# A decoder layer with product-key experts: the 512 prompt tokens taken in two chunks, the dense layer of the second placed between the expert gathers of the first

## What is computed

```
mod  = silu(c) @ w_mod + b_mod                  # shift, scale and gain, six of them
z    = modulate(rmsnorm(x)) @ w_in              # xr, gr, q, k, v, two gates
y_r  = (rglru(causal_conv(xr)) * gelu(gr)) @ w_rnn_out
y_a  = window_attention(rope(q), rope(k), v) @ w_attn_out
x1   = x + gt1 * ((sig(gate_r) * y_r + sig(gate_a) * y_a) @ w_out)
h2   = modulate(rmsnorm(x1))
s    = (h2 @ w_pq) . sub_keys                   # 8 heads, two sides of 128 keys
      per head: best 16 of each side, best 16 of the 256 sums -> 16 experts, softmax shares
out  = sum over the 128 experts of a token: share * gelu(h2 . u_tab[e]) * v_tab[e]
y    = rmsnorm(x1 + gt2 * out)
```

## Time and profile before

| | |
|---|---|
| median of 3 runs | 2475.72 us (2469.61 to 2476.45) |
| span of the profiled execution | 2483.4 us |
| busy: PE, DVE, POOL, ACT | 1922.2, 1273.5, 1287.2, 706.2 us |
| first expert gather issued | 903.87 us |
| moved by transfers | 635.52 MB, of it gathers 545.33 MB |

### The profile page before, as it was taken

How to read it: one execution, slowest core, us unless ns; L and a number is a source line. 1 busy time by engine, 2 the same in 40 slices (tenths; PEclk the granted TensorE clock), 3 DMA queues, 4 the chain that set the end, 5 groups by cost and what they waited for, 6 DMA issues and landing times.

```text
span 2483.4 us, 25659 instructions
## 1 busy us (share of the span) xinstructions
PE 1922.2 (77%) x8102; PEld 1260.9 (51%) x8102; DVE 1273.5 (51%) x2896; ACT 706.2 (28%) x1770; POOL 1287.2 (52%) x1126
## 2 busy tenths in 40 slices
PE   8899988999997986676667757757767666776676
PEld 8899888888997972232223323323223222332232
DVE  2430366434333107656656746655756655765663
ACT  1222422233223323323313323222313323323222
POOL 0221123001431346667676766767767667766663
PEclk8899988999998997888878878788888888878877
DMA  5233332112221238999999999999999998999996
GB/s 222 94 131 111 123 136 97 39 47 82 86 86 35 77 134 334 366 363 360 362 332 357 373 342 363 361 339 340 366 356 358 354 351 327 369 354 358 372 347 233
DMA packets 164900, 635.52 MB, mean 256 GB/s; under 512 B 18800, under 2 KB 19640, under 8 KB 156224
## 3 DMA queue, kind: packets, MB, share of 16 engines
q0 software_dynamic: 149760, 545.33, 58.7%
q1 hardware_dynamic: 15072, 89.24, 10.1%
HBM read 631.30 MB, written 5.20 MB: 256 GB/s over the span
## 4 chain that ended last, share of the span: by engine, by line
PE 41%; issue 19%; DVE 15%; POOL 8%; DMA 6%; another core or an unknown queue 5%; ACT 5%; POOLq 0%; DVEq 0%; ACTq 0%; SPq 0%
PE acc L722 9%; POOL arena L1443 8%; PE acc L512 6%; PE acc L513 6%; PE acc L514 6%; DVE arena L1396 6%; DMA arena<-in_u_tab,pku 5%; PE acc L528 4%; PE acc L496 3%; ACT arena L996 2%; PE acc L562 2%; ACT pk L991 1%; PE acc L631 1%; PE acc L649 1%
## 5 line engine op out<-in xcount | busy, mean ns | idle before, releaser
L722 PE MATMUL acc<-arena 128*128 128x512 f32 x2080 | 1048.5, 668 | 473.6 <-ACT arena L996 346.8
L722 PEld LDWEIGHTS acc<-arena 128*128 128x128 f32 x2080 | 442.8, 217 | 1080.7 <-issue 1078.9
L1396 DVE CUSTOM_DVE_ANT_0 arena<-arena 128x1024 f32<-128x1024 f32 x520 | 631.2, 1226 | 416.0 <-DMA arena<-in_u_tab,pku 378.4
L1443 POOL DMA_INDIRECT arena<-in_v_tab,pku x520 | 552.9, 1063 | 316.3 <-issue 157.6
L1443 POOL DMA_INDIRECT arena<-in_u_tab,pku x520 | 526.2, 1012 | 167.3 <-issue 152.2
L1460 POOL TENSOR_TENSOR w_lo<-arena,w_hi 128x1024 fp32r<-128x1024 f32 x80 | 194.6, 2437 | 682.1 <-ACT w_hi L794 682.1
L512 PE MATMUL acc<-h_hi,w_hi 128*128 128x260 f32 x992 | 292.7, 295 | 22.0 <-DVE h_lo L1101 11.7
L513 PE MATMUL acc<-h_lo,w_hi 128*128 128x260 f32 x992 | 287.9, 290 | 0.0
L514 PE MATMUL acc<-h_hi,w_lo 128*128 128x260 f32 x992 | 287.1, 289 | 0.0
L988 ACT ACTIVATE pk<-pk 128x8 f32<-128x8 f32 x65 | 13.6, 209 | 936.3 <-issue 617.6
L512 PEld LDWEIGHTS acc<-h_hi,w_hi 128*128 128x128 f32 x992 | 194.4, 196 | 25.7 <-DVE h_lo L1101 12.6
(11 more groups left out here) (230 smaller groups left out, 1863.0 us busy)
## 6 DMA issues: line engine op xcount, KB each, us to landing
arena<-w_mod SPq DMA_DIRECT2D x24, 1024.0 KB, 4.9
arena<-in_u_tab,pku POOLq DMA_INDIRECT x520
arena<-in_v_tab,pku POOLq DMA_INDIRECT x520
arena<-w_pq SPq DMA_DIRECT2D x8, 1024.0 KB, 4.7
arena<-w_xr SPq DMA_DIRECT2D x5, 1024.0 KB, 4.9
arena<-w_gr SPq DMA_DIRECT2D x5, 1024.0 KB, 4.9
arena<-w_qk SPq DMA_DIRECT2D x5, 1024.0 KB, 4.7
arena<-w_rnn SPq DMA_DIRECT2D x8, 640.0 KB, 4.0
```

Source lines behind the costliest of these rows:

```text
L722: mm = pe.matmul(y[:, h, :], diag[q][:, j, :], vt_row[j][:, h * 512:(h + 1) * 512], start=False, stop=True, skip_group_check=True)
L1396: dve.tensor_tensor_reduce(u_row[j], u_row[j], hcur, 1.0, 0.0, ALU.mult, ALU.add, dots[q][:, j:j + 1]).then_inc(s_urd, 1)
L1443: pool.indirect_dma_start(out=row, out_offset=None, in_=table, in_offset=bass.IndirectOffsetOnAxis(ap=idx, axis=0), **more).then_inc(signa ...
```

## The change

The whole order of the kernel is written out, without hardware loops. Tokens go in two chunks: A has prompt tokens 0 to 255, B has 256 to 511 and the sample tokens. The dense layer is done for A alone, up to its first expert scores, then for B, whose instructions are dealt out among the expert groups of A on every engine. Every weight but those of the modulation is read twice, in pieces of 512 KB. Rows, scores and residuals that outlive a chunk go through memory (`x_rows`, `h_rows`, `key_rows`, through three small buffers that ACT fills and SP stores) and are read back when they are needed.

The plan lists the products of PE in their order (391 of them) with a cost for each. From the first scores of A on, each expert group has four **parts**. `_limits` deals the products out so that each of the 120 parts of the first 30 groups gets an equal share of the cost up to the first half of B's scores, and each of the next 20 parts an equal share of the rest. On each engine a part is: the expert work of two of the eight rows, then the dense steps up to the limit. A step of another engine carries the number of the product that it follows, and is done in the part in which that product is. In the dealt-out stretch there are four weight buffers and two `w_hi`; before it, eight and four.

The diff rewrites nearly every line; this is its core.

```
+def _rounding():
...
+    for n, p in enumerate(SPLITS):
+        over = max(free[p], HI_AFTER[p])
+        m = min([m for m in points if m + 1 >= over]) if n >= OWN_HI + EXTRA_HI else -1
+        assert m < FIRST[p], p
+        at.append(max(m, at[-1] if at else -1))
+    return at
...
+    for (lo, hi), steps in (((PEER_FROM, HALF_WAY), HALF_STEP), ((HALF_WAY, NPRODUCTS), LAST_STEP - HALF_STEP)):
+        total, spent, at = sum(COST[lo:hi]), 0.0, lo
+        for i in range(steps * PARTS):
+            goal = total * (i + 1) / (steps * PARTS)
+            while at < hi and spent + COST[at] / 2 <= goal:
+                spent += COST[at]
+                at += 1
+            limits.append(hi if i == steps * PARTS - 1 else at)
...
+        class Course:
...
+            def until(self, limit):
+                while self.at < limit:
+                    self.at = next(self.steps, NPRODUCTS)
...
         @block.tensor
...
+            def expert_sums(g, js):
+
+                tile, part, first, last = group_of(g)
+                if js[0] == 0:
+                    pe.wait_ge(s_diag, g + 1)
+                    if first and tile:
+                        pe.wait_ge(s_yfree, tile)
+                for j in js:
+                    pe.wait_ge(s_vt[j], 16 * (g + 1))
+                    for h in range(2):
+                        mm = pe.matmul(y[:, h, :], diag[g % 2][:, j, :], vt_row[j][:, h * 512:(h + 1) * 512],
+                                       start=(first and j == 0), stop=True, skip_group_check=True)
+                    mm.then_inc(s_vrd, 1)
...
+            for g in range(GROUPS + 2):
+                for q in range(PARTS):
+                    if g:
+                        expert_sums(g - 1, (2 * q, 2 * q + 1))
+                    if g * PARTS + q < len(LIMITS):
+                        course.until(LIMITS[g * PARTS + q])
...
         @block.scalar
...
+            def round_pieces(product):
+
+                while split[0] < len(SPLITS) and ROUND_AT[split[0]] <= product:
+                    piece = SPLITS[split[0]]
+                    src = await_piece(act, piece)
+                    if HI_AFTER[piece]:
+                        act.wait_ge(s_ready, HI_AFTER[piece])
+                    act.copy(w_hi[HI_SLOT[piece]], src[:, 0:D]).then_inc(s_hi, 1)
+                    split[0] += 1
...
+            for g in range(GROUPS + 2):
+                tile, step = divmod(g - 1, 2 * PH)
+                if g > 1 and step == 0:
+                    take_sums(tile - 1)
+                if g:
+                    weights(g - 1)
...
         @block.vector
...
+                for q in range(PARTS):
+                    if g <= GROUPS:
+                        dot_products(g, (2 * q, 2 * q + 1))
...
+                    if q == 1 and g % 2 == 0 and g // 2 + 1 <= HEADS:
+                        choose(g // 2 + 1)
...
         @block.gpsimd
...
+            def gather_v(g, j):
+                if g == 0:
+                    pool.wait_ge(s_ready, EXTRA_OVER)
+                else:
+                    pool.wait_ge(s_vrd, SLOT * (g - 1) + j + 1)
...
+            def dense():
+                for n, p in enumerate(SPLITS):
+                    yield max(ROUND_AT[n], 0)
+                    hi, lo = w_hi[HI_SLOT[p]], w_lo[PIECE_SLOT[p]]
+                    pool.wait_ge(s_hi, n + 1)
+                    pool.tensor_tensor(lo, ring[PIECE_SLOT[p]][:, 0:D], hi.bitcast(F32), ALU.subtract).then_inc(s_lo, 1)
...
+            for g in range(GROUPS + 2):
+                for q in range(PARTS):
+                    for j in (2 * q, 2 * q + 1):
+                        if g <= GROUPS:
+                            gather_u(g, j)
+                        if g:
+                            gather_v(g - 1, j)
+                    if g * PARTS + q < len(LIMITS):
+                        course.until(LIMITS[g * PARTS + q])
```

More of the change, by code:

```diff
@@ L152 @@
 _plan()
+PIECES = sorted(PIECE_NO, key=PIECE_NO.get)
 SPLITS = sorted(SPLIT_NO, key=SPLIT_NO.get)
[L155 to L187, removed]
+NPRODUCTS = len(NO)
+PEER_FROM = NO[0, "keys", 0] + 1
+def _slots(order, own, extra):
+    slot, nth, after, last, count, place = {}, {}, {}, {}, {}, [0, 0]
+    for p in order:
+        late = FIRST[p] >= PEER_FROM
+        s = place[late] % (own if late else own + extra)
+        place[late] += 1
+        slot[p], after[p] = s, last.get(s, 0)
+        count[s] = count.get(s, 0) + 1
+        nth[p], last[s] = count[s], LAST[p]
+    return slot, nth, after
@@ L454, in _ @@
[L454 to L467 removed]
+            order = list(PIECES)
@@ new lines, in dense @@
+            def dense():
+                pe.wait_ge(s_cond, 1)
+                for i in range(8):
+                    yield NO[0, "mod", i]
+                    modulation(i)
+                    if i == 3:
+                        yield NO[0, "norm", 0]
+                        first_norm(0)
+                for ch in range(2):
+                    yield from chunk(ch)
+            def expert_sums(g, js):
[6 more added lines that the diff above has]
+                    pe.wait_ge(s_vt[j], 16 * (g + 1))
@@ new lines, in dense @@
+            def dense():
+                act.wait_ge(s_c, 16)
+                act.activation(cond, cT, ACT.Sigmoid).then_inc(s_sig0, 1)
+                act.wait_ge(s_par, 16)
+                first_norm_squares(0)
+                act.wait_ge(s_lam, 1)
+                act.activation(lamt[:, 1, :], lamt[:, 0, :], ACT.Exp, scale=-1.0).then_inc(s_elam, 1)
+                yield NO[0, "norm", 0]
+                root(0, 0)
+                for ch in range(2):
+                    yield from chunk(ch)
@@ new lines, in exponentials, with weights @@
+            def exponentials(head):
+                act.wait_ge(s_fv, head + 1)
+                act.activation(fexp, fv, ACT.Exp, bias=nfv, accum_out=fsum).then_inc(s_fexp, 1)
+            def weights(g):
+                tile, part, first, last = group_of(g)
+                head = g // 2
+                q = g % 2
+                if tile < TILES:
+                    act.wait_ge(s_gs, head + 1)
+                    gains, basis = gs[head % 3][:, part * SLOT:part * SLOT + SLOT], ident
+                else:
+                    act.wait_ge(s_sidx, 16 * 4)
+                    gains, basis = w_s, cst("selT")
+                act.wait_ge(s_urd, SLOT * (g + 1))
+                act.activation(gl, dots[q], ACT.Gelu).then_inc(s_gl, 1)
+                act.wait_ge(s_gl, g + 1)
@@ L1439, in _, with settled, gather @@
+            final_norm(TILES - 1)
+            add_residual(TILES)
+            final_norm(TILES)
         @block.gpsimd
         def _(pool):
-            def gather(row, table, idx, signal, read=None):
-                more = {} if read is None else {"engine_sem": read}
+            def settled():
+                pool.sem_inc(s_passed, 1)
+            def gather(row, table, idx, signal, more):
+                settled()
                 pool.indirect_dma_start(out=row, out_offset=None, in_=table,
```

2307 lines of the change are left out of this document (1334 added, 973 removed).

## The result

The changed kernel takes 3380.91 us (median of 4 runs, 3355.4 to 3390.51) where the kernel before takes 2472.66 us beside it: a ratio of 1.3653, 95% interval 1.3596 to 1.3711. The prediction said 3207 us, 2880 to 3530, slower with a chance of 0.89.

What follows compares the result with a forecast made beforehand. It took POOL, held in each remainder part until its own last gather was used, to bound the kernel: 512 (chunk A) + 20 (group 0) + 1758 (groups 1 to 29) + 925 (rest) = 3215 us profiled, 3207 forecast, range 2880 to 3530.

Steps and rivals of the forecast that it cites:

- the loop through POOL's own gathers: Dealt-out parts: POOL's remainder (`w_lo`) waits for ACT, ACT for PE's block, PE for that part's `v` gathers; 19.2 us.
- the gap on POOL: Sign in a part with a remainder: POOL idle 12 to 15 us after four gathers; waits for ACT 8 to 13 each.
- the DMA share and the clock: Signs from first gather to some 2300 us: DMA share near 0.5, clock well under 0.83; afterwards share 0.95 again.
- The price of a part: Dealt-out part with one remainder: 19.2 us (bounds 17.2 and 22); with two, 22.1; an ordinary part costs 5.9.
- The last landing: From issue of a part's last `v` gather to its use by PE: 6.2 us, from the before's 5.33 to 8.04.
- Parts without a remainder: Dealt-out parts where POOL runs on and PE sets the pace: 7.2 us each, 45 in groups 1 to 29.
- Waits in the dense layer: Groups 1 to 29: uncovered waits, such as scores to softmax to transposes and second norm; 50 us (bounds 0 and 150).
- is asked for two blocks ahead: Weight loads: a 512 KB piece lands in under 4.7 us and is requested early enough, so it was costed at nothing.
- Chunk A: Dense stage up to the first gather: PE 450, idle 50, bare choice of experts with its copy 12; total 512 us.
- Group 0 and the tail: Group 0, gathers of `u` only: 20 us; groups 30 to the end: 802 + 80 + 42.8, together 925 us.
- Rival 2: Even groups: DVE's 10.7 us choice of experts lengthens a part; 3370 to 3530 us in all; chance 0.22.
- Rival 1: Dealt-out groups: POOL isn't held, a group costs its larger budget of 29.3 us; 2228 us in all; chance 0.10.

Runs made afterwards that it cites:

- e1: Changed kernel with POOL's dense steps (the remainders) of each part done one part later; 2807.32 us, ratio 1.1353 to the kernel before.
- e2: Changed kernel with PE's dense steps of a part put ahead of its expert sums, POOL's order kept; 2788.56 us in one run.
- e3: Changed kernel with ACT rounding each weight block of the dealt-out stretch twice; 3464.9 us, ratio 1.4013 to the kernel before.
- e5: Changed kernel with POOL issuing both `v` gathers of a part ahead of both `u`; 3253.42 us, ratio 1.3083 to the kernel before.
- e8: Changed kernel with the 86 late remainders moved from POOL to DVE and PE's dense steps ahead of its expert sums; 2438.85 us, ratio 0.9814 to the kernel before.
- e9: Changed kernel with chunk B's `gate_r` pieces turning in three weight slots, `rnn` keeping the fourth, loads reordered to match; 3364.65 us, ratio 1.3519 to the kernel before.
- e4: Changed kernel with all of chunk B's dense work in the first part of group 0, nothing dealt out; 2676.42 us, ratio 1.0832 to the kernel before.
- e7: Changed kernel with POOL's remainders one part later and PE's dense steps ahead of its expert sums; 2540.84 us in one run.
- e6: Changed kernel with the 86 remainders after the first scores moved from POOL to the end of DVE's part; 2662.91 us, ratio 1.0728 to the kernel before.

## Why the prediction was right

The forecast was the loop through POOL's own gathers, and seven runs (e1, e2, e3, e5 to e8) lengthen, shorten, stretch or open that loop, each with the sign that it gives. Of the signs that were named, the gap on POOL (12.49 us in the part shown), the DMA share and the clock came as told; the waits average 13.4 us (1045.8 over 78), just above the 8 to 13. Point by point:

- **The price of a part.** 19.2 us was taken. Of the 64 parts with one remainder, the 43 that directly follow another part with a remainder have a mean of 19.8 and a median of 19.6. Those with two: 22.91 in the median against 22.1. The counts, 64, 7 and 45, are those of the trace.
- **The last landing.** 6.2 us was taken from rows of a full queue. In the part shown, PE's first weight load of the second row ended a wait for the gather at 1973.83, 5.95 us after that gather began; the second row's sums then took 2.75 to the block, where 2.7 was taken. The first gather of the same part, with little else moving (DMA share 0.26 from 1964 to 1966 us), was used by DVE 4.36 us after its start, the second by PE after 5.71. What counts in the loop is the last of four. The Trainium skill, DMA: Bandwidth & Descriptors, section Anatomy of one DMA, gives 3.2 us for 512 KB (an estimate from its formula, as in the prediction). With POOL's 0.94 us ahead of it that is 4.1, close to the first gather and short for the later ones; that these share the transfers with those before them would explain it, but no run here tries it.
- **Parts without a remainder.** The failed detail is 7.2 us: POOL passes them in 5.37 on average. It runs ahead, and the backlog of PE falls into the next part with a remainder: the 21 parts with one remainder that follow a part without have a mean of 27.0 us, against 19.8 for the 43. The 45 parts are 82 us short of their price, the 21 are 164 above theirs. So the 7.2 came back in the parts behind, with another 81 us, most of the excess of the next point.
- **Waits in the dense layer.** "I take 50 (bounds 0 and 150)" was too small: groups 1 to 29 took 1833 us against 1758, so over the prices of the parts the excess is 125. The step that failed here is that a weight piece "is asked for two blocks ahead" and so costs nothing. It holds where one kind of block follows another, not where `gate_r` and `rnn` alternate; that is some 22 us, by e9. The rest, at the convolution and the attention, wasn't tested by a run of its own.
- **Chunk A.** 512 us was taken, 547.65 measured. The terms that were too small are PE's busy time, 450 taken and 470.27 measured, and its idle time, 62 taken with the bare choice of experts and 77 measured, inside the bounds. e4 shows the same for chunk B: its 366 us of PE and the 28 left over from A, 394, came to 448.60 busy and 85 idle. Half of the tokens is not half of the time.
- **Group 0 and the tail.** Group 0 took 29.4 us for 20. Groups 30 to the end took 979 us for 925: late groups 24.7 us each where 23.6 was taken from the kernel before, and 60 us from the last group's first gather to the end. Here `u` and `v` gathers alternate where POOL ran a group of `v` ahead before; whether that is the reason wasn't tried. The same 29 groups, with no dense work left in them, take 23.7 to 24.5 us each in the profiles of the experiments that keep this order, so part of the 1.1 us is what one profile differs from the next.

Together: 36 (A) + 9 (group 0) + 75 (groups 1 to 29) + 54 (the rest) = 174 us over the 3215 of the sum, against a span of 3388.7. All four terms came out longer, so none made up for another.

Some of the prediction's sums don't follow from their own terms, though the measured time lies inside the range either way. The low end of a part is 3.7 + 5.33 + 1.85 + 3.0 + 3.6 = 17.5 us and not 17.2. The high end adds up to about 3610 and not 3530: 542 + 20 + 2115 for groups 1 to 29 + 942 for the late groups, less 8. By a landing 2.06 us shorter in 77 parts the sum is 3056 and not 3065.

**Rival 2** gave 3370 to 3530, and 3381 lies in it, but it isn't what happened. It needs long parts in even groups after the choice of experts. Among the 43 parts above, those in the second and third place of even groups have means of 19.8 and 19.7 us, those in odd groups 19.2 and 19.3: half a microsecond, not 10.7. Over all parts of groups 1 to 29, the long ones too, even groups exceed the prices of their parts by 4.9 us a group and odd ones by 3.8, so the long parts aren't its work either. DVE waits 785.2 us for gathers in that stretch, and the choice seems to fit into that. **Rival 1**, that POOL isn't held, named the right condition, a part with a remainder under about 9 us. e7 reaches 8.46 in the median, though 11.2 in the mean, and in e8 POOL has no remainder in that stretch. Its 2228 us was still too hopeful: in e8 a group of the overlapped stretch takes 34.2 us (991.29 / 29) against the 29.3 of its budget, with PE idle 0.19 of the time, and the chunking's 175 us was not in it.

## What to carry to other kernels

When work is dealt out among engines with strict lists, draw the ring: from an engine's wait back through whoever releases it, and see whether it passes through something that the same engine issued in the same step. If it does, each step costs the whole way round, however idle all engines are, and no budget of busy times shows it; the cure is a step of distance somewhere in the ring (e1, e2, e7). Another engine for the waiting instruction (e6) moved the ring to that engine, and was worth most with such a step (e8). Where neither an engine nor the transfers are near full in a long stretch (here 0.53 at most and 0.48), read the waits as a ring and not one by one. Halving the tokens of a dense layer doesn't halve its time: here it added 175 us before any overlap could begin to pay.

## What the runs showed of the hardware that was not expected

- DVE's remainder is twice as fast as POOL's: 1.22 us (86 of them in e8) against 2.40 us (160 in the changed kernel), for the same 128x1024 subtraction.
- A subtraction of 128x264 on DVE that takes 0.43 us alone takes 2.45 beside POOL's remainder:

```profile
1980.68 0.43 DVE L1596 TENSOR_TENSOR arena<-arena 128x264 f32<-128x264 f32 x1
1981.15 0.30 DVE L1597 CAST m_hi<-arena 128x264 fp32r<-128x264 f32 x1
1981.48 2.45 DVE L1598 TENSOR_TENSOR m_lo<-arena,m_hi 128x264 fp32r<-128x264 f32 x1
```

  These are DVE's rows of the part shown above; POOL's remainder runs from 1981.31 to 1983.65, and DVE's subtraction ends at 1983.93. In the same stretch of e8, where POOL does no subtraction, all eight of that line take 0.43 us; in the changed kernel seven of the eight take 2.45 to 2.46. The Trainium skill, SBUF — State Buffer, section Who interferes with whom, says that a DVE operation with two operands from SBUF and a GpSimd operation that reads SBUF contend for a shared port, which one of them holds alone; these rows agree. So the move to DVE in e6 and e8 took these two costs away together with POOL's part in the loop, and what each was worth there isn't separated; in e1, e2 and e7 the remainders stay on POOL.
